# RMS norms of a two-layer diffusion block: sums, roots and reciprocals with tokens on partitions, and two modulation blocks at another place

## Chip, core and metric

The kernel runs on one NeuronCore of one Trainium2 chip. The metric is the device time of one execution in microseconds (us), lower is better. TensorE (PE) multiplies, VectorE (DVE) and ScalarE (ACT) do elementwise work, GpSimd (POOL) and SyncE (SP) issue transfers. In the profile PEld is TensorE's weight load, which overlaps PE.

## Reference

The reference is a two-layer backbone over 512 latent and 256 context tokens of width 1024, all in float32. Cut to what the change touches, it is:

```python
def rms_norm(x, g):
    y = x * rsqrt(mean(x * x, axis=-1) + EPS)
    return y * g

for l in range(2):
    sh1, sc1, g1, sh2, sc2, g2 = split(cond @ w_mod[l] + b_mod[l], 6)   # the modulation; likewise for the context
    u = rms_norm(h, norm1_g[l]) * (1 + sc1) + sh1
    y = token_mixers(u, ...)           # neighbourhood, grouped and differential attention, convolution
    h = h + g1 * (y @ w_out[l])
    u = rms_norm(h, norm2_g[l]) * (1 + sc2) + sh2
    h = h + g2 * expert_choice_ffn(u, ...)   # router, top tokens of each of 16 experts, gated products
return rms_norm(h, final_g)
```

The context tokens take part in layer 0 throughout; in layer 1 they pass only the first norm and the input projection. So the kernel has five norms: the first and second norm of layer 0 and the first of layer 1 over 512 (latent) and 256 (context) tokens where they are needed, the second of layer 1 and the final one over the latent tokens alone.

## The kernel before

**Layout.** The residual stream `h` and the normed `u` keep channels on partitions: 8 slices `k` of 128 channels by 768 tokens (512 latent, then 256 context). The sum over channels of a norm is therefore a sum over partitions. It is made on TensorE: ACT squares a slice into `ex`, and PE multiplies by `ones_d`, a 128x128 matrix of 1/1024, and accumulates the 8 slices in PSUM (`norm_sum`, L543; for the second norm six of the slices are added by DVE first, so that L781 and L784 are two products; `final_sum`, L549). Because every column of `ones_d` is the same, the result has the mean of each token on all 128 partitions. ACT then takes the root of all of it (`norm` of the scalar block, L1051, and L1294 in the final norm), DVE the reciprocal (`invert`, L1356, and L1707), both on 128 partitions by 512 and 256 tokens, and DVE multiplies `h` by the gain and by this array (L1366, L1710: 8 slices of the latent tokens, then 8 of the context). ACT adds the shift (L1063) and PE takes the slices up one after the other: at L599 as the first token tiles of the input projection, at L802 as the router's product.

**Order of work.** Each engine has a program written out by hand. PE's sequence around the second norm of layer 0 is: output projection (L759), the two sum products, the modulation blocks `MOD_N` (numbers 13 and 14), the router (L802, L808), the transposes of `u` for the gather's table in memory (L825), the blocks `MOD_R` (15 to 20), which run beside DVE's search for the top tokens (L1601 to L1605), the transpose of the found rows (L841), the blocks `MOD_G` (21 to 23), and then the first gathered tokens (L863, L866) and the expert products (L886, L892 in layer 0, L880 in layer 1). A modulation block is `mod_products` (L516), a copy on ACT, and `mod_pick` (L527), whose products have a moving operand of 4 columns.

**Weights.** SP loads all weights as blocks of 2 MB in one fixed order (`STREAM`, then the experts' 12 blocks for each pair of experts), each into the next free one of six to nine slots. `fill` (L446) waits until PE has released the slot's last block. So a modulation block that PE takes up later is released later, and so is the slot that the next block in the order needs. For layer 0 the third expert block also waits for the first gather:

```python
if l == 0 and j == 2:
    sp.wait_ge(sig["e_g", 0], 32)
```

The slots of the stretch around the second norm, from the tables of the kernel, are: block 13 in slot 3, 14 in 1, 15 in 4, 16 in 5, 17 in 0, 18 in 2, 19 in 3, 20 in 1, 21 in 4, 22 in 5, 23 in 0, the first two expert blocks in 2 and 3. Slots 4 and 5 lie in attention's buffers and come free when attention is done. Block 18 waits for the last block of the output projection to be released.

**The gather.** GpSimd fetches the tokens of an expert pair with two indirect transfers (`take_rows`, L1757 latent, L1760 context), once DVE has the rows (L1619, L1623). PE transposes what comes (`gather`, L863, L866), ACT copies it out, and the pair's products follow.

## Time and profile before

| | |
|---|---|
| three runs, us | 2116.8, 2120.46, 2122.64 (median 2120.46) |
| the profiled execution, us | 2119.77 |
| its span in the profile, us | 2118.0 |
| mean granted TensorE clock | 0.972 |
| busy in the span: PE, PEld, DVE, ACT, POOL | 91%, 59%, 32%, 24%, 16% |
| HBM read | 506.88 MB |

The span runs from the first to the last profiled instruction; 1.8 us of the execution lie around it. A busy PE is not PE at its peak, since matmuls are pipelined.
### The profile page before, as it was taken

The page shows a single profiled execution, that of the slowest core. Times are in us where ns is not written, and L with a number is a line of the kernel's source. Part 1 is how long each engine was busy: PE and PEld are TensorE (multiplying, and loading weights), DVE is VectorE, ACT ScalarE, POOL GpSimd, SP SyncE. Part 2 cuts the span into 40 slices and gives each one's busy share as a digit, 9 for nine tenths or more (in the row PEclk, how much of TensorE's full clock was granted, in tenths as well). Part 3 has the DMA queues.
Part 4 walks back from the last instruction along what each step waited for, and adds up shares of the span by engine and source line. Part 5 has one row for each costly group of instructions (what it writes and reads, how often), then busy time and mean ns, then how long its engine had stood idle before and what let it go on. Part 6 is the DMA issues. An engine that isn't in the chain of part 4 may idle for free.

```text
span 2118.0 us, 40681 instructions
## 1 busy us (share of the span) xinstructions
PE 1933.4 (91%) x18156; PEld 1247.9 (59%) x18156; DVE 687.1 (32%) x1329; ACT 507.8 (24%) x1118; POOL 344.1 (16%) x200
## 2 busy tenths in 40 slices
PE   6999989989879999999998899979893999988896
PEld 4656656755557666666665546557642666655553
DVE  3085367762520000000002444367635111111113
ACT  4001246640402111211111311246602111110012
POOL 0004037730000111001110004038600000000000
PEclk9999989999989999999999999989996999999999
DMA  9431110062499999999996321110035999999994
GB/s 397 179 137 40 40 40 2 2 266 92 179 378 420 405 401 409 406 411 402 399 387 255 144 75 40 40 41 1 8 153 220 386 426 427 426 428 427 426 428 183
DMA packets 43738, 525.46 MB, mean 248 GB/s; under 512 B 5232, under 2 KB 5232, under 8 KB 13488
## 3 DMA queue, kind: packets, MB, share of 16 engines
q1 hardware_dynamic: 35136, 492.21, 56.2%
q0 software_dynamic: 6992, 25.43, 3.8%
q10 hardware_dynamic: 1440, 5.24, 0.6%
q8 instruction: 144, 2.36, 0.4%
q14 instruction: 26, 0.21, 0.0%
HBM read 506.88 MB, written 15.99 MB: 247 GB/s over the span
## 4 chain that ended last, share of the span: by engine, by line
PE 69%; DMA 11%; DVE 7%; issue 5%; PEld 3%; POOL 2%; ACT 2%; ACTq 0%; SPq 0%; DVEq 0%; PEldq 0%; POOLq 0%
PE ps L886 14%; PE ps L581 12%; PE ps L880 9%; PE ps L892 7%; PE ps L759 6%; PE ps L702 4%; PE ps L599 4%; DMA ring<-in_w_exp 3%; PE ps L1001 2%; PE ps L720 2%; POOL arena L1740 2%; PE ps L736 2%; DMA u<-in_w_exp 2%; DMA arena<-in_w_exp 2%; DVE arena L1515 2%
## 5 line engine op out<-in xcount | busy, mean ns | idle before, releaser
L581 PE MATMUL ps<-u,ring 128*128 128x512 f32 (+1 forms) x800 | 276.9, 507 | 0.0
L1740 POOL TENSOR_SCALAR arena<-arena,rsum 128x768 f32<-128x768 f32 (+3 forms) x120 | 216.5, 1819 | 291.0 <-DVE rsum L1535 241.1
L581 PEld LDWEIGHTS ps<-u,ring 128*128 128x128 f32 x800 | 151.7, 190 | 123.7 <-issue 115.7
L1664 DVE SCALAR_TENSOR_TENSOR arena<-arena,ps 128x512 f32<-128x512 f32 x40 | 27.4, 685 | 538.3 <-ACT arena L1226 538.3
L886 PE MATMUL ps<-ring,arena 128*32 128x256 f32 x3200 | 184.0, 381 | 6.2 <-PE ps L892 3.9
L880 PE MATMUL ps<-ring,arena 128*64 128x256 f32 x1408 | 161.1, 385 | 16.1 <-DMA ring<-in_w_exp 9.4
L880 PE MATMUL ps<-arena 128*64 128x256 f32 x1344 | 151.1, 380 | 13.8 <-DMA arena<-in_w_exp 10.9
L1150 ACT ACTIVATE arena<-arena,negmax 128x768 f32<-128x768 f32 (+3 forms) x160 | 129.8, 812 | 112.2 <-DVE arena L1515 91.4
L886 PEld LDWEIGHTS ps<-ring,arena 128*32 128x32 f32 x3200 | 117.5, 110 | 64.2 <-issue 13.4
L880 PEld LDWEIGHTS ps<-ring,arena 128*64 128x64 f32 x1408 | 105.0, 139 | 70.2 <-DMA ring<-in_w_exp 16.1
L702 PE MATMUL ps<-arena 64*128 64x256 f32 (+4 forms) x576 | 118.2, 518 | 26.9 <-DVE arena L1515 15.5
L759 PE MATMUL ps<-u,ring 128*128 128x512 f32 (+1 forms) x384 | 137.8, 521 | 0.0
L892 PE MATMUL ps<-ring,arena 128*32 128x256 f32 x1600 | 136.9, 382 | 0.0
L880 PEld LDWEIGHTS ps<-arena 128*64 128x64 f32 x1344 | 98.7, 137 | 62.9 <-DMA arena<-in_w_exp 16.9
L886 PE MATMUL ps<-arena 128*32 128x256 f32 x2304 | 132.0, 380 | 0.5 <-PE ps L892 0.5
L892 PE MATMUL ps<-arena 128*32 128x256 f32 x1152 | 129.3, 383 | 0.0
L1226 ACT ACTIVATE arena<-ps 128x512 f32<-128x512 f32 x40 | 24.0, 599 | 438.4 <-PE ps L880 223.4
L599 PE MATMUL ps<-ring,u 128*128 128x256 f32 (+1 forms) x576 | 112.8, 354 | 10.5 <-ACT u L1063 6.1
L1515 DVE TENSOR_SCALAR_CACHE_REDUCE arena<-ps 128x768 f32<-128x768 f32 (+1 forms) x128 | 100.3, 821 | 65.3 <-PE ps L702 64.4
L599 PEld LDWEIGHTS ps<-ring,u 128*128 128x128 f32 x576 | 96.8, 195 | 29.5 <-issue 13.0
L759 PEld LDWEIGHTS ps<-u,ring 128*128 128x128 f32 x384 | 73.0, 190 | 64.5 <-issue 61.2
L886 PEld LDWEIGHTS ps<-arena 128*32 128x32 f32 x2304 | 86.4, 110 | 36.8 <-issue 1.2
(203 smaller groups left out, 2281.5 us busy)
## 6 DMA issues: line engine op xcount, KB each, us to landing
ring<-in_w_exp SPq DMA_DIRECT2D x94, 2048.0 KB
arena<-in_w_exp SPq DMA_DIRECT2D x78, 2048.0 KB, 28.2
ring<-in_w_mod SPq DMA_DIRECT2D x20, 2048.0 KB
u<-in_w_exp SPq DMA_DIRECT2D x20, 2048.0 KB, 28.0
ring<-in_w_in SPq DMA_DIRECT2D x10, 2048.0 KB
ring<-in_w_out SPq DMA_DIRECT2D x4, 2048.0 KB
arena<-in_w_mod SPq DMA_DIRECT2D x4, 2048.0 KB, 11.9
u_rows<-arena ACTq DMA_DIRECT2D x10, 512.0 KB, 2.9
```

What stands on the lines that cost most here:

```text
L581: mm = pe.matmul(ps[:, bb, 0:n], w[:, k, P * ct:P * ct + P], u[:, k, t0:t0 + n], start=k == 0, stop=k == KD - 1)
L599: mm = pe.matmul(ps[:, 4 + nv % 2, 0:cn], u[:, k, P * t:P * t + P], w[:, k, c0:c0 + cn], start=k == 0, stop=k == KD - 1)
L702: mm = pe.matmul(psf[:, c0:c0 + k1 - k0], qk[r0:r0 + rn, qt, q0:q0 + P], qk[r0:r0 + rn, kt, k0:k1], start=True, stop=True, tile_position=( ...
L720: mm = pe.transpose(ps[:, 3 + i % 4, P * x:P * x + P], ex[:, (2 * p + e) % N_EX, P * (y % n):P * (y % n) + P], cst("ident"))
L736: mm = pe.matmul(ps[64 * e:64 * e + 64, 7, 0:P], val[:, kt, v0:v0 + HD], pt[:, i % N_PT, c0:c0 + P], start=x == 0, stop=x == len(ktiles) - ...
L759: mm = pe.matmul(ps[:, 4 + 2 * (i % 2) + c, 0:n], w[:, k, P * (i % 4):P * (i % 4) + P], u[:, k, t0:t0 + n], start=k == 0, stop=k == KD - 1)
L880: mm = pe.matmul(ps[64 * c:64 * c + 64, bank, cols:cols + 256], stationary(k, i), w[i][:, k, 256 * c:256 * c + 256], start=k == 0, stop=k ...
L886: mm = pe.matmul(ps[g:g + 32, bank, cols:cols + 256], stationary(k, i)[:, 32 * r:32 * r + 32], w[i][:, k, 256 * c:256 * c + 256], start=k ...
L892: mm = pe.matmul(ps[g:g + 32, bank, cols:cols + 256], stationary(k, 2 + e), w[e][:, k, 256 * c:256 * c + 256], start=k == 0, stop=k == KD - 1,
L1150: act.activation(ex[:, i % N_EX, 0:kn], ex[:, i % N_EX, 0:kn], ACT.Exp, scale=-1.0, bias=negmax[:, i % 16:i % 16 + 1], accum_out=sums[:, i ...
L1515: dve.tensor_scalar(dst[:, 0:kn], src, -1.0, 3.0e38, ALU.mult, ALU.min, accum_out=low).then_inc(s["s_max"], 1)
L1740: pool.tensor_scalar(e0, e0, rsum[:, c0:c0 + 1], None, ALU.mult).then_inc(s["p_norm"], 1)
```

## The change

It does three things. Each norm's sum is made with the squares as stationary operand, 128 tokens at a time, against 4 columns of `ones_d`, so that the mean of each token lies on its own partition, in one column for every 128 tokens (`token_sums`); ACT's root and DVE's reciprocal then run on 128 partitions by 6 or 4 elements (`inv_t`), and PE spreads each column over all partitions by transposing it, broadcast 128 times (`spread`). DVE's multiplication reads the result from PSUM (`spread_to`). Before the squares of the first norm of each layer and of the final norm ACT takes a root of a constant. And `MOD_N` is gone: blocks 13 to 18 are now `MOD_R`, beside the search for the top tokens, and 19 to 23 are `MOD_G`, after the transpose of the found rows, while the first gather is under way. The order of the loads and their slots is unchanged.

```diff
+        inv_t = mx6
+        def spread_to(c):
+            return ps[:, 0, CTX:CTX + CTX] if c else ps[:, 1, 0:LAT]
...
-        MOD_N, MOD_R, MOD_G = range(13, 15), range(15, 21), range(21, 2 * MOD_BLOCKS)
+        MOD_R, MOD_G = range(13, 19), range(19, 2 * MOD_BLOCKS)
+        MOD_AHEAD = 15
...
-                    if key == ("mod", MOD_R[0]):
+                    if key == ("mod", MOD_AHEAD):
                         sp.wait_ge(sig["dn_sq", 0], 1)
...
+            def token_sums(squares, tiles, start, stop):
+                for t in range(tiles):
+                    mm = pe.matmul(ps[:, 0, 4 * t:4 * t + 4], squares[:, P * t:P * t + P], cst("ones_d")[:, 0:4],
+                                   start=start and t == 0, stop=stop and t == tiles - 1)
+                return mm
-            def norm_sum(which, l, parts, ks=range(KD)):
+            def norm_sum(l, ks=range(KD)):
                 for k in ks:
...
-                    for t0, n, c in parts:
-                        mm = pe.matmul(ps[:, c, 0:n], cst("ones_d"), ex[:, k % 2, t0:t0 + n],
-                                       start=k == 0, stop=k == KD - 1)
-                    mm.then_inc(sig[which + "_mm", l], 1)
+                    token_sums(ex[:, k % 2, :], TL + TC, k == 0, k == KD - 1).then_inc(sig["n1_mm", l], 1)
...
+            def spread(tiles):
+                for t in range(tiles):
+                    mm = pe.transpose(spread_to(t // TL)[:, P * (t % TL):P * (t % TL) + P],
+                                      inv_t[:, t:t + 1].to_broadcast([P, P]), cst("ident"))
+                return mm
...
                 if l == 0:
-                    norm_sum("n1", l, parts_of(l))
+                    norm_sum(l)
+                    pe.wait_ge(sig["n1_inv", l], since("n1_inv", l) + 1)
+                    spread(TL + TC).then_inc(sig["n1_rb", l], 1)
                     pe.wait_ge(sig["cond_done"], 1)
                     modulation(range(4))
...
-                if l == 0:
-                    pe.wait_ge(sig["o_ev", l], KD)
-                    for m in MOD_N:
-                        mod_products(m, 4 + m % 2)
-                    pay()
-                    for m in MOD_N:
-                        mod_pick(m, 4 + m % 2, MOD_TOK["out"][m % 2])
+                pe.wait_ge(sig["n2_inv", l], since("n2_inv", l) + 1)
+                spread(nt).then_inc(sig["n2_rb", l], 1)
...
             def norm(which, l, parts):
...
+                if which == "n1":
+                    act.activation(inv_t[:, 7:8], cst("eps"), ACT.Sqrt)
...
-                act.activation(ex[:, 2, 0:t1], bank2(0, t1), ACT.Sqrt, bias=cst("eps")).then_inc(sig[which + "_root", l], 1)
+                act.activation(inv_t[:, 0:nt], ps[:, 0, 0:4 * nt].rearrange("p (t x) -> p t x", x=4)[:, :, 0], ACT.Sqrt,
+                               bias=cst("eps")).then_inc(sig[which + "_root", l], 1)
...
-                link(dve.reciprocal(ex[:, 2, t0:t0 + n], ex[:, 2, t0:t0 + n]), ("self", l))
+                dve.reciprocal(inv_t[:, 0:nt], inv_t[:, 0:nt]).then_inc(sig[which + "_inv", l], 1)
...
                         dve.scalar_tensor_tensor(u[:, k, t0:t0 + n], h[:, k, t0:t0 + n], gain[:, i, k, c:c + 1],
-                                                 ex[:, 2, t0:t0 + n], ALU.mult, ALU.mult).then_inc(sig[which + "_pre", l], 1)
+                                                 spread_to(c), ALU.mult, ALU.mult).then_inc(sig[which + "_pre", l], 1)
```

The final norm is changed in the same way, with four tiles of tokens.

At the start of the program PE had 16 products of 512 and 256 columns (L543) ahead of the first four modulation blocks (L516, L527); the last two of them head the piece. Before:

```order
L543 MATMUL ps<-arena,const 128x512
L543 MATMUL ps<-arena,const 128x256
L516 MATMUL ps<-ring,cond_w 32x256 x32
L527 MATMUL ps<-const,arena 128x4 x2
L516 MATMUL ps<-ring,cond_w 32x256 x16
```

And now, where L548 is the sum, L564 the spread, L522 and L533 the modulation's products and picks:

```order
L548 MATMUL ps<-const,arena 128x4 x48
L564 MATMUL ps<-const,mx 128x128 x6
L522 MATMUL ps<-ring,cond_w 32x256 x32
L533 MATMUL ps<-const,arena 128x4 x2
L522 MATMUL ps<-ring,cond_w 32x256 x16
```

The spread now stands between the sum and the modulation blocks, and it waits for ACT and DVE.

From the second norm of layer 0 to the first gathered tokens (L863, which is L873 in the change) PE had:

```order
L784 MATMUL ps<-arena,const 128x256
L516 MATMUL ps<-ring,cond_w 32x256 x32
L527 MATMUL ps<-const,arena 128x4 x4
L802 MATMUL ps<-u,small 32x256 x24
L808 MATMUL ps<-const,arena 128x96 x2
...
L841 MATMUL ps<-const,arena 128x48 x4
L516 MATMUL ps<-arena,cond_w 32x256 x32
L527 MATMUL ps<-const,arena 128x4 x2
L516 MATMUL ps<-ring,cond_w 32x256 x16
L527 MATMUL ps<-const,arena 128x4 x4
L863 MATMUL ps<-const,arena 128x128 x4
```

And now (L812 is the router, L851 the transpose of the rows):

```order
L548 MATMUL ps<-const,arena 128x4 x12
L564 MATMUL ps<-const,mx 128x128 x6
L812 MATMUL ps<-u,small 32x256 x24
L818 MATMUL ps<-const,arena 128x96 x2
...
L851 MATMUL ps<-const,arena 128x48 x4
L522 MATMUL ps<-ring,cond_w 32x256 x32
L533 MATMUL ps<-const,arena 128x4 x2
L522 MATMUL ps<-arena,cond_w 32x256 x16
L533 MATMUL ps<-const,arena 128x4 x2
L522 MATMUL ps<-arena,cond_w 32x256 x16
L533 MATMUL ps<-const,arena 128x4 x2
L522 MATMUL ps<-ring,cond_w 32x256 x16
L533 MATMUL ps<-const,arena 128x4 x4
L873 MATMUL ps<-const,arena 128x128 x4
```

Two blocks of 16 products left the place ahead of the router, and five instead of three now stand behind the transpose of the rows.

## Rows read from the trace of the kernel before

**Rows 1.** The page's part 4, the chain that ended last, by engine
```profile
PE 69%; DMA 11%; DVE 7%; issue 5%; PEld 3%; POOL 2%; ACT 2%; ACTq 0%; SPq 0%; DVEq 0%; PEldq 0%; POOLq 0%
```

**Rows 2.** Waits of PE, 612 to 1080 us: engine, waited for, total, times, longest
```profile
PE ps L863 <- issue: 8.4, 1, 8.4
```

**Rows 3.** Chain in order of time, last pairs of layer 1: start us, us, what
```profile
1868.96 36.73 DMA ring<-in_w_exp
...
2087.14 3.70 PE ps L880 x32
```

**Rows 4.** Timeline, short operations: start us, us, engine, line, operation, [idle before]
```profile
569.57 1.04 PE L825 MATMUL ps<-const,u 128*128 128x128 f32 x8
571.30 0.19 DVE L1592 RECIPROCAL mx<-mx 128x6 f32<-128x6 f32 x1
583.05 0.61 PE L527 MATMUL ps<-const,arena 128*128 128x4 f32 x4
```

**Rows 5.** Timeline, start of the program
```profile
14.80 12.90 PE L543 MATMUL ps<-arena,const 128*128 128x512 f32 x32 [14.80 <-ACT arena L1046]
26.03 1.28 ACT L1051 ACT_TABLE_LOAD   x1
27.64 3.66 PE L516 MATMUL ps<-ring,cond_w 128*32 128x256 f32 x64
38.45 8.55 ACT L1063 ACTIVATE u<-u,mod 128x512 f32<-128x512 f32 x16 [1.90 <-DVE u L1366]
39.46 8.86 PE L599 MATMUL ps<-ring,u 128*128 128x256 f32 x32 [2.24 <-DMA ring<-in_w_in]
```

**Rows 6.** One line of the kernel, L543: records, ns min/median/max, first and last start
```profile
L543 PE MATMUL ps<-arena,const x64: 379/592/1193, 14.8 to 1189.7; 128*128 128x512 f32 x32, 128*128 128x256 f32 x32
```

**Rows 7.** Timeline, second norm of layer 0
```profile
551.04 1.56 PE L784 MATMUL ps<-arena,const 128*128 128x512 f32 x4 [0.43 <-ACT arena L1040]
552.64 0.90 ACT L1051 ACTIVATE arena<-ps,const 128x768 f32<-128x768 f32 x1 [1.65 <-PE ps L784]
553.64 3.35 DVE L1356 RECIPROCAL arena<-arena 128x512 f32<-128x512 f32 x1 [3.32 <-ACT arena L1051]
557.03 5.39 DVE L1366 SCALAR_TENSOR_TENSOR u<-h,gain,arena 128x512 f32<-128x512 f32 x8
562.33 1.75 DVE L1356 RECIPROCAL arena<-arena 128x256 f32<-128x256 f32 x1
```

**Rows 8.** Timeline, from the loads of blocks 21 on to the first expert products
```profile
581.75 2.73 SPq L446 DMA_DIRECT2D arena<-in_w_mod  x2
...
600.45 1.93 PE L516 MATMUL ps<-ring,cond_w 128*32 128x256 f32 x32 [2.04 <-DMA ring<-in_w_mod]
...
611.91 1.09 PE L863 MATMUL ps<-const,arena 128*128 128x128 f32 x4 [8.36 <-issue]
...
617.64 8.55 PE L886 MATMUL ps<-ring,arena 128*32 128x256 f32 x128 [1.28 <-issue]
```

**Rows 9.** DMA issues, 595 to 598 us: what, engine, times, us to landing
```profile
arena<-u_rows,rows_c POOLq DMA_INDIRECT x1, 14.6
```

**Rows 10.** Stretches: us, PE, PEld, DVE, ACT, POOL busy, PE clock, DMA share, GB/s
```profile
20.00:25.00 5.00, 5.00 (x17) 2.87 (x16) 0.00 (x0) 3.37 (x4) 0.00 (x0) 1.00 1.00 426
...
606.00:612.00 6.00, 0.09 (x1) 0.12 (x2) 0.00 (x0) 0.00 (x0) 0.00 (x0) 0.55 0.90 273
...
1605.30:1610.20 4.90, 3.72 (x30) 2.86 (x28) 1.58 (x8) 3.15 (x7) 0.00 (x0) 1.00 0.94 399
```

**Rows 11.** Timeline, first norm of layer 1
```profile
1191.13 3.35 DVE L1356 RECIPROCAL arena<-arena 128x512 f32<-128x512 f32 x1 [3.31 <-ACT arena L1051]
...
1205.90 3.29 PE L599 MATMUL ps<-ring,u 128*128 128x256 f32 x14 [0.42 <-ACT arena L1096]
```

**Rows 12.** Timeline, second norm of layer 1 and final norm
```profile
1592.76 0.69 ACT L1051 ACTIVATE arena<-ps,const 128x512 f32<-128x512 f32 x1 [1.22 <-PE ps L784]
...
2109.96 5.39 DVE L1710 SCALAR_TENSOR_TENSOR u<-h,small,arena 128x512 f32<-128x512 f32 x8
```

66 lines of the change are left out of this document (30 added, 36 removed).

## The prediction

> **What bounds the kernel now.** I read the chain of waits first. PE holds 69% of it and transfers 11% [rows 1], so the question of every stage is whether PE or the weight stream ends last. In the experts of layer 0 PE waited for no transfer: its only long idle stretch from 612 us on is the 8.4 us ahead of the first gathered tokens [rows 2]. That stage moves as a whole with its start. In layer 1 the chain of the last pairs hangs on a 36.73 us wait for an expert block, and after the last of these PE has 3.70 us of work [rows 3]: there the stream sets the end, and a gain ahead of it counts only as far as it brings the first release of a slot earlier. The first expert product there releases the first slot, so the second norm of layer 1 still counts. The timeline around each norm then gives the terms. A microsecond there is one at the end unless something covers it.
>
> **The price of the pieces.** A sum of one slice is 12 records now (6 tiles), where it was 4 long ones. Four records with 4 columns take 0.61 us [rows 4], and each further record comes as fast as in a group of transposes, 8 in 1.04 us, so (1.04 - 0.61) / 4 = 0.107 us. Twelve take 0.61 + 8 x 0.107 = 1.47 us, and four of the old records take 1.56 [rows 7]. The sums come out even. The spread is 12 records, 1.04 + 4 x 0.107 = 1.47 us, for six tiles and 1.04 for four. Root and reciprocal of 6 columns: DVE's on 128x6 takes 0.19 [rows 4], and I give ACT the same. From the end of the sum to DVE's first multiplication it was 557.03 - 552.60 = 4.43 us [rows 7]; now it is 0.19 + 0.19 + 1.47 and four hand-overs of 0.1 (553.64 after 552.64 + 0.90), 2.25 in all. **Saved: 2.2 us** for the latent tokens, and 1.75 us more for the context tokens, whose reciprocal [rows 7] stood between the two halves. DVE reads PSUM instead; its operations of this size on PSUM and on SBUF take about the same (5.39 / 8 = 0.67 us for those from SBUF), and I take 0.2 us per norm for it. At the end of a norm with context 3.8 us are saved.
>
> **First norm of layer 0: a loss of 3.3 us.** ACT's table load of 1.28 us stood after the squares, while PE finished its sums (26.03 to 27.31; PE was done at 27.70) [rows 5]. The root of a constant puts it ahead of the first square, with 0.2 us of its own: +1.5. The modulation blocks followed the sums at once, at 27.64 [rows 5]; now the spread stands ahead of them, with root, reciprocal and hand-overs, +2.2. DVE's root and reciprocal were hidden here, so nothing comes back: DVE cannot multiply before the blocks give the gain. The projection's first product waited for its weights until 39.46, some 0.35 us after ACT's first slice (38.45 + 0.67) [rows 5]; that is the only cover. 1.5 + 2.2 - 0.35 = **+3.3**. The weights follow: block 0 is released 3.7 later, and the load behind it starts with an empty queue, but it had been queued behind others before, so it lands before the first slice is ready.
>
> **Second norm of layer 0 and the moved blocks: 0.** All that hangs on the norm comes 3.8 earlier: router, search, the first release of `MOD_R` (581.75 to 577.95 [rows 8]) and the gather. But the stream behind `MOD_R` is longer. Before, SP had loaded blocks 19 and 20 while PE was in the norm; now their slots are freed only in `MOD_R`. A block is 2.10 MB at 426 GB/s [rows 10], 4.93 us. The third block asked for after 581.75 was there at 600.45, when PE went on [rows 8]: 18.7 = 3 x 4.93 + 3.9. The last block of `MOD_G` is now the fifth: 577.95 + 5 x 4.93 + 3.9 = 606.5. The gather's 192 rows of 4 KB (0.79 MB, 1.9 us at that rate) now run beside these loads, which makes it 608.4. Then come the last block's products and picks, 603.56 - 600.45 = 3.1 us, and the gathered tokens' transposes and copies, 617.64 - 611.91 = 5.7 [rows 8]: 617.2 against 617.64. The gather lands earlier: 597.19 - 3.8 + 14.6 = 608.0 [rows 9], and no longer decides. Because the share of the gather could be felt by more than its bytes (its landing took 14.6 us for 1.9 us of bytes), I round the 0.4 of gain away. The two blocks' own 3.66 us on PE cost nothing at either place: ahead of the router PE waited anyway, and now they fall into the 8.4 us of idle.
>
> **First norm of layer 1: -2.8.** DVE starts 2.2 earlier. The third token tile of the projection (1205.90 [rows 11]) waits for ACT, which copies the first tile out only after the last context slice; that is 3.8 earlier, but PE must also do its two first tiles, which start 2.2 earlier and run 0.6 less long once the clock is up. The table load moves to where ACT waits for the experts' last sums.
>
> **Second norm of layer 1: -2.4.** End of sum to multiplication was 1592.73 to 1596.94 (the reciprocal is as long as in [rows 11], the root 0.69 [rows 12]), 4.2; with four tiles it is 0.19 + 0.19 + 1.04 + 0.4 = 1.8.
>
> **Final norm: -2.6.** The same, 4.4 to 1.8; DVE's multiplications started at 2109.96 [rows 12], and all that follows stays.
>
> Sum: +3.3 + 0 - 2.8 - 2.4 - 2.6 = **-4.5 us** on 2119.77, so 2115.3. The profiled execution is 0.7 under the median of the runs; the prediction is **2116.0 us**. About 0.3% (6.4 us) is what a measurement of this kernel can tell from no change, so most of this case lies within it.
>
> **The rivals.**
>
> *A. Slower: the clock stays low through the sums at the start.* The first record of L543 took 1193 ns where the median is 592 [rows 6], so PE begins at its low level (1.2 GHz) and rises to 2.4 while it streams 512 columns without a pause. The new sums stream 4 columns per weight load. If that does not raise the clock, 8 x 12 records take double, 96 x 0.213 = 20.5 us instead of 12.9: +7.6. The spread adds 1.4, and the first two modulation blocks (3.66 us [rows 5]) start low, +2.3. Total 11.3 more: **2127.3**. For it: no row shows a cold PE that rises on such work. Against it: PE would have a record in flight all the time, and in the stretch 1605.30 to 1610.20, which holds only transposes with pauses between, the clock was 1.00 [rows 10]. It decides if the clock does not rise within the first half of the sums. 0.2.
>
> The Trainium skill, page "TensorE: Matmul & The Clock Gate", section "Part 4: PE-mode transpose", says that transposes do not count as busy for the clock. By that rule the four later spreads would run at half the rate, 1.4 + 1.4 + 1.0 + 1.0 = 4.8 us more, and the time would be 2120.8. The stretch just named, with 1.00 over transposes alone, disagrees with it; 0.04.
>
> *B. Faster: the weights are no limit before the first experts.* Then the 3.8 us of the second norm stay. Moreover PE would be at work shortly before the gathered tokens, and not at the 0.55 of the stretch 606 to 612 [rows 10]; the transposes (1.09 us for four records against 1.04 for eight [rows 4, 8]) and the first products would save 1.6. 2116.0 - 5.4 = **2110.6**. It needs the fifth block by 603. Against it is the arithmetic of the queue; for it, that the third block's 3.9 us of delay is one block's reading, and that the gather may share better than I take it. 0.25.
>
> *C. The gather is felt more.* The fifth block lands at 611, not 608.4, because its slowest part waits behind the rows, PE is cold again by then, and the experts start 3 us later: **2119**. 0.15.
>
> *D. The new sums are not even.* If weight loads of squares are not hidden (0.19 us each instead of 0.107), each slice takes 0.8 longer, eight slices at the start and eight before layer 1: 13 more, **2129**. The rows of the four-column picks speak against it. 0.03.
>
> The rest, 0.33, is the forecast itself.
>
> **How the numbers follow.** The forecast's own range is 2112.5 to 2119.5 (the start 1 us either way with the phase of the clock's rise, each norm half a microsecond, the moved blocks two). B reaches below and A above; the range that leaves out no more than 2 in 10 is **2109 to 2127.5**. Faster by over 0.3% is below 2114.1: nearly all of B and a quarter of the forecast, 0.32. Slower is over 2126.8: 0.6 of A, D, and a little of C, 0.17. The rest is 0.51.
>
> **What would show it.** In the profile after: DVE's first multiplication 2.2 us after the last sum of a norm with six tiles and 1.8 with four; a table load before the first square and the projection's first product at 42.8; the last block's products ahead of the first gathered tokens at about 608, ended by a transfer; layer 1's projection 2.8 nearer to its last sum; in the last layer the first release of a slot 2.4 nearer to the norm. A span of PE records of 20 us at the start shows A. A first expert product before 616 (617.64 with the 3.3 of the start is 620.9) shows B. The prediction is wrong if the start loses nothing, or if the expert stage of layer 0 begins to wait for transfers.

## The result, and the profile after

The changed kernel takes **2135.14 us** (median of 5 runs, 2131.4 to 2138.47), the kernel before beside it 2120.46: ratio 1.0070, 95% interval 1.0055 to 1.0084. It is slower by 0.7%, outside the forecast range (2109 to 2127.5). On two other chips (runs e12 and e16 below) it came out at 1.0062 both times (2135.83 and 2134.40 us).

| | before | after |
|---|---|---|
| profiled execution, us | 2119.77 | 2135.14 |
| its span, us | 2118.0 | 2133.3 |
| mean granted clock | 0.972 | 0.968 |
| PE busy in the span | 91% | 92% |

The chain by engine has lost DVE time, 5% for 7% [rows 1], as the change meant, but PE and transfers have more.

```profile
PE 71%; DMA 12%; DVE 5%; issue 5%; PEld 3%; POOL 2%; ACT 2%; ACTq 0%; SPq 0%; DVEq 0%; PEldq 0%; POOLq 0%
```

**The start.** The timeline of the changed kernel, which answers to [rows 5]. L548 is the sum, L1066 the root, L564 the spread, L522 the modulation products, L617 the projection:

```profile
13.53 1.28 ACT L1048 ACT_TABLE_LOAD   x1
...
15.90 20.61 PE L548 MATMUL ps<-const,arena 128*128 128x4 f32 x96 [15.90 <-ACT arena L1061]
...
36.55 0.27 ACT L1066 ACTIVATE mx<-ps,const 128x6 f32<-128x6 f32 x1 [4.28 <-PE ps L548]
36.91 0.19 DVE L1373 RECIPROCAL mx<-mx 128x6 f32<-128x6 f32 x1 [22.64 <-ACT mx L1066]
...
37.16 1.54 PE L564 MATMUL ps<-const,mx 128*128 128x128 f32 x6 [0.65 <-DVE mx L1373]
38.63 5.77 PE L522 MATMUL ps<-ring,cond_w 128*32 128x256 f32 x64
...
52.41 1.20 PE L617 MATMUL ps<-ring,u 128*128 128x256 f32 x3 [2.10 <-ACT u L1076]
```

The 96 records of the sums take 20.61 us, 0.213 each, where 0.107 was worked out, and the modulation products behind them 5.77 instead of 3.66. The projection's first product comes at 52.41 instead of 39.46: 12.95 us of the 15.3 by which the spans differ are lost before anything else has begun. The durations of the records show that the engine was at its low level, 1.2 GHz, until about 43 us; the column PEclk, the granted clock, does not:

```profile
core 0: us, PE busy (x) PEld busy (x) DVE busy (x) ACT busy (x) POOL busy (x), PEclk, DMA share, GB/s
...
20.00:24.00 4.00, 4.00 (x21) 4.00 (x20) 0.00 (x0) 1.09 (x2) 0.00 (x0) 1.00 0.98 418
```

Twenty-one records in 4 us, all of it busy, are the low rate, and beside it stands 1.00; e5 below has 1.00 beside 21 records in 4 us and then beside 38. So at the start of an execution a reader goes by the duration of the records and not by this column.

**The second norm of layer 0.** This answers to [rows 7]; DVE's multiplication is L1381.

```profile
566.13 1.47 PE L548 MATMUL ps<-const,arena 128*128 128x4 f32 x12
568.09 2.29 PE L548 MATMUL ps<-const,arena 128*128 128x4 f32 x12 [0.49 <-ACT arena L1055]
570.42 0.27 ACT L1066 ACTIVATE mx<-ps,const 128x6 f32<-128x6 f32 x1 [2.38 <-PE ps L548]
570.79 0.19 DVE L1373 RECIPROCAL mx<-mx 128x6 f32<-128x6 f32 x1 [3.41 <-ACT mx L1066]
...
571.03 1.54 PE L564 MATMUL ps<-const,mx 128*128 128x128 f32 x6 [0.65 <-DVE mx L1373]
572.62 2.72 DVE L1381 SCALAR_TENSOR_TENSOR u<-h,gain,ps 128x512 f32<-128x512 f32 x4 [1.64 <-PE ps L564]
```

The first twelve records take the 1.47 us of the forecast. In the second twelve the clock falls, and they take 2.29. From their end (570.38) to the multiplication it is 2.24 us, and the forecast was 2.25. The spread in it is six records, one for each tile, not the twelve of the forecast, and they run at the low level: 1.54 us, where six take 0.87 at the full clock (e5 and e15 below).

**From there to the experts.** The chain, and PE's timeline, which answer to [rows 8]:

```profile
605.34 21.72 DMA ring<-in_w_mod
```
```profile
627.11 3.36 PE L522 MATMUL ps<-ring,cond_w 128*32 128x256 f32 x32 [2.90 <-DMA ring<-in_w_mod]
...
636.40 1.08 PE L896 MATMUL ps<-ring,arena 128*32 128x256 f32 x8 [1.12 <-issue]
```

The last modulation block lands 21.7 us after it was asked for (13.9 before), and the experts start at 636.40, 18.8 us behind before's 617.64.

**Layer 1 and the end.** The first norm of layer 1 (the first two rows), its second norm and the final norm answer to [rows 11, 12]:

```profile
1213.94 0.19 DVE L1373 RECIPROCAL mx<-mx 128x6 f32<-128x6 f32 x1 [2.72 <-ACT mx L1066]
...
1215.83 3.38 DVE L1381 SCALAR_TENSOR_TENSOR u<-h,gain,ps 128x512 f32<-128x512 f32 x5 [1.70 <-PE ps L564]
```
```profile
1612.62 0.26 ACT L1066 ACTIVATE mx<-ps,const 128x4 f32<-128x4 f32 x1 [1.15 <-PE ps L548]
...
1614.37 5.36 DVE L1381 SCALAR_TENSOR_TENSOR u<-h,gain,ps 128x512 f32<-128x512 f32 x8 [1.21 <-PE ps L564]
```
```profile
2125.30 5.36 DVE L1722 SCALAR_TENSOR_TENSOR u<-h,small,ps 128x512 f32<-128x512 f32 x8 [1.21 <-PE ps L564]
```

The delay against the kernel before, read from both timelines at the same instructions: first product of the projection +12.95 us, first attention product +15.39, output projection +17.0, first expert product +18.76, first wide scatter product +23.15, layer 1's first transposed projection tile +19.98, expert stage of layer 1 +17.04, final multiplication +15.34. So the stretches that hold the two norms of layer 1 and the final one gain (3.2, 2.9 and 1.7 us), and all others lose. Between the first expert product and the first wide scatter product of layer 0, where the change has edited nothing on PE, the delay grows by 4.4 us.

### The profile page after: what moved, and what is told of

It reads as the page before. It is cut to its first block, busy times and chain, and to the rows that moved or that the text cites. A ratio compares the mean times of both kernels' runs of the same rounds, so it can differ in the third digit from the quotient of the medians.

```text
span 2133.3 us, 41142 instructions
## 1 busy us (share of the span) xinstructions
PE 1957.4 (92%) x18386; PEld 1277.7 (60%) x18386; DVE 665.6 (31%) x1326; ACT 505.7 (24%) x1121; POOL 342.3 (16%) x200
## 4 chain that ended last, share of the span: by engine, by line
PE 71%; DMA 12%; DVE 5%; issue 5%; PEld 3%; POOL 2%; ACT 2%; ACTq 0%; SPq 0%; DVEq 0%; PEldq 0%; POOLq 0%
PE ps L896 14%; PE ps L599 12%; PE ps L890 9%; PE ps L902 7%; PE ps L777 6%; PE ps L617 4%; PE ps L720 4%; DMA ring<-in_w_exp 3%; PE ps L1011 2%; PE ps L738 2%; PE ps L548 2%; POOL arena L1752 2%; PE ps L754 2%; DMA u<-in_w_exp 2%; DMA arena<-in_w_exp 2%
## 5 line engine op out<-in xcount | busy, mean ns | idle before, releaser
L896 PEld LDWEIGHTS ps<-ring,arena 128*32 128x32 f32 x3200 | 116.8, 111 | 65.4 <-issue 13.7
L617 PE MATMUL ps<-ring,u 128*128 128x256 f32 (+1 forms) x576 | 112.0, 352 | 5.5 <-ACT u L1076 3.8
L617 PEld LDWEIGHTS ps<-ring,u 128*128 128x128 f32 x576 | 96.3, 194 | 24.3 <-issue 8.6
```

Of the source, the lines that this page charges most:

```text
L617: mm = pe.matmul(ps[:, 4 + nv % 2, 0:cn], u[:, k, P * t:P * t + P], w[:, k, c0:c0 + cn], start=k == 0, stop=k == KD - 1)
L896: mm = pe.matmul(ps[g:g + 32, bank, cols:cols + 256], stationary(k, i)[:, 32 * r:32 * r + 32], w[i][:, k, 256 * c:256 * c + 256], start=k ...
```

## The experiments

Two theories stood at the beginning. **Theory 1:** the loss is the start; the sums of 4 columns do not raise the clock, and root, reciprocal, spread and table load stand in series. **Theory 2:** the loss lies in the moved blocks and the transfers behind them. Ratios are against the kernel before on the same chip. "Scatter to tile" is the time from the first 512-column scatter product to layer 1's first transposed projection tile, in which the first norm of layer 1 lies; it and the two starts are from the one profiled execution. Each group of runs was made on one chip: e1 to e4, e5 to e8, e9 to e12, and e13 to e16; the kernel before has one median for the first result and one for each of these groups.

| run | median us | ratio (interval) | projection starts | L0 experts start | scatter to tile |
|---|---|---|---|---|---|
| before | 2120.5; 2121.7, 2122.3, 2122.4, 2121.4 | 1 | 39.5 | 617.6 | 50.7 |
| changed (first / e12 / e16) | 2135.1 / 2135.8 / 2134.4 | 1.0070 / 1.0062 / 1.0062 | 52.4 / 52.6 / 51.9 | 636.4 / 635.7 / 634.9 | 47.5 / 53.9 / 47.5 |
| e1 old first norm | 2125.17 | 1.0011 (0.9999, 1.0023) | 39.5 | 620.3 | 58.9 |
| e2 PE warmed ahead | 2136.88 | 1.0079 (1.0063, 1.0095) | 50.2 | 630.9 | 47.6 |
| e3 blocks back | 2137.38 | 1.0073 (1.0057, 1.0089) | 52.5 | 633.0 | 47.5 |
| e4 = e1 and e3 | 2120.87 | 0.9997 (0.9984, 1.0009) | 39.7 | 621.2 | 55.6 |
| e5 128 columns | 2118.04 | 0.9985 (0.9973, 0.9997) | 41.7 | 621.4 | 46.9 |
| e6 e5, start reordered | 2117.31 | 0.9981 (0.9972, 0.9991) | 39.9 | 619.7 | 46.9 |
| e7 e6, blocks back | 2111.53 | 0.9952 (0.9938, 0.9965) | 40.2 | 621.1 | 47.0 |
| e8 e4, 128 columns | 2109.07 | 0.9940 (0.9927, 0.9953) | 39.7 | 623.4 | 46.9 |
| e9 before, blocks moved | 2130.13 | 1.0031 (1.0019, 1.0044) | 39.3 | 623.4 | 50.7 |
| e10 128 columns at the start only | 2131.26 | 1.0044 (1.0030, 1.0058) | 42.0 | 627.0 | 53.9 |
| e11 start reordered, 4 columns | 2133.81 | 1.0059 (1.0045, 1.0072) | 48.5 | 631.4 | 47.6 |
| e13 128 columns but at the start | 2127.12 | 1.0033 (1.0021, 1.0045) | 52.5 | 631.6 | 46.9 |
| e14 blocks back, once more | 2133.84 | 1.0058 (1.0038, 1.0078) | 51.9 | 635.0 | 53.9 |
| e15 e5, blocks back | 2114.79 | 0.9964 (0.9951, 0.9977) | 42.6 | 622.9 | 46.9 |

### e1: the first norm of layer 0 as before

```
+                    if l == 0:
+                        for t0, n, c in parts_of(l):
+                            mm = pe.matmul(ps[:, c, 0:n], cst("ones_d"), ex[:, k % 2, t0:t0 + n],
+                                           start=k == 0, stop=k == KD - 1)
...
-                    spread(TL + TC).then_inc(sig["n1_rb", l], 1)
```

> The changed kernel, with the first norm of layer 0 put back as it was before the change (ones times 512 columns, root and reciprocal of 768 columns, no spread); the other four norms and the moved modulation blocks stay changed. Theory 1 (the start is the loss: the four-column sums run at 1.2 GHz and the spread and table load stand in series): the projection's first product is back at about 39.5 us instead of 52.41, everything behind it is at least 12.9 us earlier, 2135.1 - 12.9 = 2122, and nearer 2118 if the 2.4 us more at 97 to 131 us and the 1.7 us more in the attention only come from the shifted phase of the clock. Theory 2 (the loss lies in the stretch of the moved blocks and behind it, where the transfers set the time, and the start's delay would be absorbed there): the experts of layer 0 start hardly earlier than 636.4, and the time stays above 2130.

Measured: 2125.17 us, ratio 1.0011, and the projection starts at 39.55. About ten of the fifteen us come back, so theory 1 has the main part, but not the 13 to 17 that it forecast, and theory 2 falls as the main cause. The new thing is in the last column: 58.9 us from scatter to tile, 8 more than before the change, in a stretch that theory 1 held for won.

### e2: a warm PE ahead of the sums

```
+                    for i in range(12):
+                        pe.matmul(ps[:, 7, :], cst("ones_d"), const[:, 0:512], start=True, stop=True)
                     norm_sum(l)
```

> The changed kernel with 12 matmuls of ones times 512 columns of the constants into an unused bank of PSUM, on PE ahead of its first sum, in the 9.9 us in which it waited for the input. Nothing else differs, so this changes the clock alone. Theory 1a (the clock is the larger part of the start's loss, and four-column sums hold a clock that is up): the 96 records of the sums take about 10.5 us instead of 20.61, the products of the first modulation blocks 3.66 instead of 5.77, the projection's first product comes at about 40.5 instead of 52.41, and the time is about 2123. Theory 1b (four-column sums let even a raised clock fall): the sums start at 0.107 us a record and turn to 0.213 on the way, and the gain is 2 to 6 us, 2129 to 2133. Theory 2 (the start's delay is absorbed later): same as the changed kernel, 2135.

The stretches of this kernel around its sums, which run from 18.47 to 34.12:

```profile
14.00:18.00 4.00, 4.00 (x10) 1.71 (x9) 0.29 (x2) 2.54 (x4) 0.00 (x0) 1.00 1.02 438
...
20.00:22.00 2.00, 2.00 (x20) 2.00 (x20) 0.00 (x0) 1.50 (x2) 0.00 (x0) 1.00 1.03 442
22.00:24.00 2.00, 2.00 (x19) 2.00 (x19) 0.00 (x0) 1.01 (x3) 0.00 (x0) 0.94 1.00 426
24.00:26.00 2.00, 2.00 (x11) 2.00 (x10) 0.00 (x0) 0.77 (x1) 0.00 (x0) 0.50 0.99 426
...
30.00:32.00 2.00, 2.00 (x11) 2.00 (x11) 0.00 (x0) 0.00 (x0) 0.00 (x0) 0.50 0.88 377
```

The wide products raise the clock; the sums begin at it, twenty records in 2 us, and at 23.8 us (the 0.94 of its stretch), with PE busy in 2.00 of 2.00 us and a record always in flight, it falls to the low level and stays there to the end of the sums. That is the mechanism of theory 1b: these records, though the profile counts them as busy, do not hold the clock. Its time did not come: the projection starts 2.2 us earlier (50.16), but the median, 2136.88, is not below the changed kernel's, where 2129 to 2133 was forecast. The profiled execution (2129.75) is the fastest of the six, and it would be wrong to read a gain from it. Because the fall came here from a clock that was up, it may come in other long rows of such records too.

### e3 and e4: the blocks back, alone and with the old first norm

```
-        MOD_R, MOD_G = range(13, 19), range(19, 2 * MOD_BLOCKS)
+        MOD_N, MOD_R, MOD_G = range(13, 15), range(15, 21), range(21, 2 * MOD_BLOCKS)
...
+                    for m in MOD_N:
+                        mod_products(m, 4 + m % 2)
```

> The changed kernel with the two modulation blocks (13 and 14) put back into the second norm of layer 0, behind its spread; all five norms stay changed. Theory 1 (the start is the loss, and the blocks' move costs what the ledger of the traces shows, the 3.1 us that the norm had gained and 1.7 more): the experts of layer 0 start 3 to 5 us earlier than 636.40, and the time is 2130 to 2132. Theory 2 (the moved blocks are the main loss): more than 8 us faster, under 2127. Theory 3 (the stream of weights sets the experts' start whichever stage the two blocks are in): within 1 us of 2135.1.

> Both edits at once: the first norm of layer 0 and the two modulation blocks as before the change, the other four norms changed. Theory 1: the loss of the start goes (13 to 17 us) and that of the blocks too (3 to 5), which leaves the gains of the later norms, 2135.1 - 15 - 4 = 2116, and 2112 to 2119 in all; this would be faster than the kernel before (2120.5) by the norms' 2.9 + 2.9 + 1.7 us and what the second norm of layer 0 keeps. Theory 2 (the later norms gain nothing net): equal to the kernel before, 2120.5.

e3 gained nothing (1.0073), as only the third theory had it; but that theory's reason, that the weights set the experts' start at either place, does not fit, since the experts start 3.4 us earlier in its profile (633.04), itself the fastest of its six executions. e4 only equals the kernel before (0.9997), the time of its theory 2, although four of its norms are shorter. Its scatter-to-tile stretch took 55.6 us. In e12, a further execution of the changed kernel, the same stretch can be seen in rows. PE's timeline there, L1023 being the wide scatter product:

```profile
1199.04 1.02 PE L1023 MATMUL ps<-arena 128*128 128x512 f32 x2
1199.90 2.74 PE L548 MATMUL ps<-const,arena 128*128 128x4 f32 x24
...
1203.98 2.56 PE L548 MATMUL ps<-const,arena 128*128 128x4 f32 x12
...
1209.10 7.68 PE L548 MATMUL ps<-const,arena 128*128 128x4 f32 x36
```
```profile
1200.00:1204.00 4.00, 4.00 (x30) 3.36 (x29) 1.14 (x2) 1.68 (x2) 0.00 (x0) 0.97 1.02 438
1204.00:1208.00 4.00, 4.00 (x16) 3.56 (x15) 1.14 (x2) 0.84 (x1) 0.00 (x0) 0.50 0.13 53
```

Twenty-four records take 2.74 us, then the clock falls within the sums and 36 take 7.68, which are 4.08 where it does not fall. Of ten profiles with four-column sums in layer 1, five show this (e1, e4, e10, e12, e14), and scatter to tile takes 53.9 to 58.9 us in them, 47.5 to 47.6 in the other five. In those five the clock was lost too, only later: the spread right behind the sums ran at the low level in all ten, 1.51 to 1.52 us for its six records. The first changed profile:

```profile
1214.27 1.51 PE L564 MATMUL ps<-const,mx 128*128 128x128 f32 x6 [0.74 <-DVE mx L1373]
```

### e5: 128 columns instead of 4

```
-                    mm = pe.matmul(ps[:, 0, 4 * t:4 * t + 4], squares[:, P * t:P * t + P], cst("ones_d")[:, 0:4],
-                                   start=start and t == 0, stop=stop and t == tiles - 1)
+                    mm = pe.matmul(psf[:, P * t:P * t + 128], squares[:, P * t:P * t + P], cst("ones_d")[:, 0:128],
+                                   start=start and t % TL == 0, stop=stop and t in (TL - 1, tiles - 1))
```

> The changed kernel with 128 columns of ones instead of 4 as the moving operand of every sum (each tile's sum stands 128 times in PSUM; the root reads one column of each). Nothing else differs. The transposes of the spread, 128 columns each, take 0.107 us a record at 2.4 GHz as the four-column sums do, so the sums should cost the same at that level. Theory 1 (four columns leave the clock low at the start, and let it fall in the sums of layer 1; 128 columns raise and hold it): the sums at the start take about 13 us instead of 20.61, the projection's first product comes at about 43 instead of 52.41, the 24 records of the sums of layer 1 take 2.7 us in whatever execution is profiled, and the time is 2115 to 2120, some 17 us under the changed kernel. Theory 2 (any group of short records with a weight load each leaves the clock low, however wide): start as in the changed kernel, 20.6 us, and the time stays at 2135. Theory 3 (128 columns cost twice as much as 4): the sums take over 20 us at either level, and the time is 2135 or more.

The start of this kernel:

```profile
15.98 12.60 PE L548 MATMUL ps<-const,arena 128*128 128x128 f32 x96 [15.98 <-ACT arena L1061]
29.23 0.87 PE L564 MATMUL ps<-const,mx 128*128 128x128 f32 x6 [0.65 <-DVE mx L1373]
30.03 3.66 PE L522 MATMUL ps<-ring,cond_w 128*32 128x256 f32 x64
...
41.71 9.30 PE L617 MATMUL ps<-ring,u 128*128 128x256 f32 x32 [2.10 <-ACT u L1076]
```

and its stretches there:

```profile
16.00:20.00 4.00, 4.00 (x21) 4.00 (x22) 0.00 (x0) 1.42 (x2) 0.00 (x0) 1.00 0.98 418
20.00:24.00 4.00, 4.00 (x38) 4.00 (x38) 0.00 (x0) 2.43 (x3) 0.00 (x0) 1.00 1.02 438
```

The same 96 records with the same weight loads. The first four microseconds hold 21 of them, as in the changed kernel; the next four hold 38 where that one holds 21. Thirty-two times the columns cost nothing (12.60 us, against 20.61) and the clock rises. The median is 2118.04 us, as theory 1 had it (2115 to 2120), 17 under the changed kernel and faster than the kernel before by 0.15% (0.03 to 0.27). Theories 2 and 3 fall. The last 36 records of layer 1's sums, and the spread behind them:

```profile
1193.46 4.18 PE L548 MATMUL ps<-const,arena 128*128 128x128 f32 x36
...
1198.38 0.84 PE L564 MATMUL ps<-const,mx 128*128 128x128 f32 x6 [0.74 <-DVE mx L1373]
```

That is 4.18 us in each of the six profiles with 128 columns there (e5 to e8, e13, e15), and scatter to tile takes 46.9 to 47.0: no fall in the sums in six of six, where four columns had it in five of ten, and the spread at the full clock (0.84 us) in six of six, where it was at the low one in ten of ten.

### e6 and e7: the serial rest of the start, and the blocks

```
-                if which == "n1":
+                if which == "n1" and l:
                     act.activation(inv_t[:, 7:8], cst("eps"), ACT.Sqrt)
...
                     norm_sum(l)
-                    pe.wait_ge(sig["n1_inv", l], since("n1_inv", l) + 1)
-                    spread(TL + TC).then_inc(sig["n1_rb", l], 1)
                     pe.wait_ge(sig["cond_done"], 1)
                     modulation(range(4))
+                    pe.wait_ge(sig["n1_inv", l], since("n1_inv", l) + 1)
+                    spread(TL + TC).then_inc(sig["n1_rb", l], 1)
```

> The kernel with sums of 128 columns, and two more edits at the start: the root of a constant ahead of the first square only in layer 1, and the spread behind the first four modulation blocks instead of ahead of them. Theory 1 (the remaining loss of the start is serial: 1.5 us for the table load, 2.2 for the spread): the projection's first product comes at 39.5 to 40.5, 3 us ahead of the kernel with 128 columns alone, and the time is 2 to 3 us under it. Theory 2 (this loss is absorbed by the waits for weights behind it): the same time as with 128 columns alone.

> As the kernel before this one, and the two modulation blocks back in the second norm of layer 0. Theory 1 (moving the blocks gave back the 3 us that the second norm had gained, since the queue of weights ends later): 1 to 4 us faster than with the blocks moved, the experts of layer 0 starting 2 us or more ahead of 617.64. Theory 3 (the blocks' place makes no difference): the same within 1 us.

The order brings the projection's start from 41.71 to 39.87, but only 0.7 us of time with overlapping intervals: between its two theories e6 decides nothing. The blocks' return is worth 5.8 us, and the intervals (0.9972 to 0.9991, 0.9938 to 0.9965) do not touch; that is more than the 1 to 4 that e7 forecast. Its profile shows it elsewhere than expected: the experts start at 621.1 where e7 forecast less than 615.6. From the start of the output projection to the first expert product it is 1.6 us shorter than in e6, and from there to layer 0's scatter 2.8 us.

### e8: e4 with 128 columns

> The kernel with the first norm of layer 0 and the two blocks as before the change, now with sums of 128 columns in the other four norms. With four columns it came out equal to the kernel before (2120.87 us against 2121.7), though its later norms are shorter; in its profiled execution the clock fell in the sums of layer 1, and the stretch from the scatter to the projection lost 5 us. Theory 1 (this fall is what ate the norms' gain): with 128 columns the sums of layer 1 run at 2.4 GHz throughout, and the time is 4 to 7 us under the four-column version, 2114 to 2117. Theory 2 (the fall there comes by chance with any kind of sum): equal to it, 2121.

2109.07 us, ratio 0.9940: the same kernel with 128 for 4 columns in four norms is 11.8 us faster than e4, more than the 4 to 7 of theory 1 (they ran on different chips; by the ratios it is 12.1). It is the fastest of the study, **0.6% under the kernel before** (0.47 to 0.73). Its profiled execution (2116.48) is the slowest of its six, so nothing is read here from its stages alone. Against e7 (2111.53) the intervals overlap: with 128 columns the old and the new first norm of layer 0 can't be told apart.

### e9 to e12: each part by itself

> The changed kernel itself, as the measure for the three runs beside it: 2134 to 2137 us, ratio 1.007 as before. If the loss at the start is fixed and only the falls of the clock in the sums of layer 1 come by chance, its runs should lie in two heaps some 8 us apart.

> The changed kernel with sums of 128 columns in the first norm of layer 0 alone; the other four norms keep 4 columns. Theory 1: the start gives back 10.7 us (the projection's first product at 41.7), the falls of the clock in the sums of layer 1 stay possible, so the time is 10 to 12 us under the changed kernel, 2124 to 2126, and some 6 us above the 2118 of the kernel with 128 columns in all norms. Theory 2 (the start is the whole of the clock's cost): 2118, as with 128 columns in all norms.

> The changed kernel, sums of 4 columns, with the root of a constant ahead of the first square only in layer 1 and the spread behind the first four modulation blocks. This takes away the serial part of the start's loss alone. Theory 1 (serial 3.3 us, the clock the other 9 to 10): the projection's first product at 49 to 50 instead of 52.41, and 2 to 4 us faster than the changed kernel. Theory 2 (the start's loss is serial in the main): more than 8 us faster.

> The kernel before with only the two modulation blocks moved; all five norms as before. Theory 1 (the last block of the gather's wait lands some 22 us after it is asked for instead of 14, because two more blocks are queued, and the norm gives nothing to pay for it): the experts of layer 0 start at 620 to 623 instead of 617.64, and the time is 2 to 5 us over the kernel before, 2124 to 2126. Theory 3 (the blocks' place makes no difference): within 1 us of the kernel before. Theory 4 (in the old place their products and copies lay on the path to the router): 1 to 3 us faster than before.

e12's six runs (2129.0, and 2134.1 to 2138.5) are no two heaps, and its profile with the fall is as long as the first one without: the fall in layer 1 is one of several that move between executions.

e10 takes 128 columns at the start alone. The projection starts at 42.0, yet only 4.6 us come back, and its interval still overlaps that of e12. In its profile the clock fell again behind the start, in the second norm of layer 0, ahead of the experts and in the sums of layer 1:

```profile
556.00:566.00 10.00, 7.75 (x36) 5.23 (x38) 5.29 (x9) 4.59 (x8) 0.00 (x0) 0.51 0.45 185
611.00:631.00 20.00, 15.75 (x120) 9.33 (x116) 0.46 (x5) 2.51 (x6) 1.86 (x2) 0.50 1.00 416
```

The second of these stretches begins in the gather's wait, where the kernel before has a low stretch too (0.55 [rows 10]), and whether the narrow sums have a part in it no run shows. e11, the serial part alone, gives some 4 us at the projection's start and 2.0 in the median, where 2 to 4 were expected; the intervals of e11 and e12 overlap almost wholly, so that the 2.0 are not shown.

e9 was made from the kernel before: its old norms, and the two blocks in the gather's wait. Forecast 2 to 5 us over the kernel before, measured 7.7 by the medians and 6.6 by the ratio (1.0031, interval 1.0019 to 1.0044): four of its eleven executions lie at 2123.1 to 2126.5 and seven at 2129.4 to 2133.0, and the profiled one is of the seven. PE's timeline, L517 being the modulation product, L880 the expert product:

```profile
607.66 3.64 PE L517 MATMUL ps<-arena,cond_w 128*32 128x256 f32 x32 [3.93 <-DMA arena<-in_w_mod]
...
614.05 3.40 PE L517 MATMUL ps<-ring,cond_w 128*32 128x256 f32 x32 [1.80 <-DMA ring<-in_w_mod]
...
623.40 8.81 PE L880 MATMUL ps<-ring,arena 128*32 128x256 f32 x124 [1.12 <-issue]
```

against e7, where the blocks are back (its modulation product is L522, its first transpose of gathered tokens L880):

```profile
603.36 3.62 PE L522 MATMUL ps<-ring,cond_w 128*32 128x256 f32 x32 [1.91 <-DMA ring<-in_w_mod]
...
615.48 1.08 PE L880 MATMUL ps<-const,arena 128*128 128x128 f32 x4 [7.33 <-issue]
```

With the blocks moved the gathered tokens follow the last block's products at once, and PE waits for that block; with the blocks back PE has idled for 7.33 us when the tokens come. The last block lands 22.4 us after it is asked for in e9, 13.7 in e7 and 13.9 in the kernel before. The queue has become the limit of this stage.

### e13 to e16: width by place on one chip

> The changed kernel with sums of 128 columns in every norm but the first of layer 0, which keeps 4. Theory 1a (the clock in the later sums costs as much as at the start, by falls in the two long rows of short records, layer 1's first norm above all, and in the second norm of layer 0 ahead of the router): with 128 columns at the start alone 4.6 us came back of 17.7, so here 10 to 13 us come back, 2123 to 2126. Theory 1b (what the start lost is lost however the rest runs, and the 4.6 us were small by the chance of the clock's falls behind it): 5 us or less come back, 2130 to 2133.

> The changed kernel with the two blocks back in the second norm of layer 0, sums of 4 columns, once more beside the changed kernel itself. Theory 1 (the blocks' place costs 6 us at any width, hidden in the first run by few runs and another chip): 4 to 7 us faster than the changed kernel beside it. Theory 2 (with four columns the sums of the second norm let the clock fall ahead of the router, and the blocks' products behind the spread then run at the low level and hold the router up, which eats the gain): the same as the changed kernel within 2 us.

> Sums of 128 columns in all norms, the two blocks back in the second norm of layer 0, the order at the start as in the changed kernel. With the other order at the start the blocks' return gave 5.8 us (2117.31 to 2111.53). Theory 1: the same here, 2118.0 - 5.8 = 2112, ratio to the kernel before 0.9955. Theory 2 (it hung on the order at the start): 2116 or more.

> The changed kernel itself on the chip of the three runs beside it: 2135 to 2137 us, ratio 1.006 to 1.007.

128 columns everywhere but at the start (e13) give 7.3 us of the changed kernel's 2134.4, at the start alone (e10) 4.6, everywhere (e5) about 17. Neither of e13's theories is met. By these medians the parts do not add, but each has an interval of two to three us to either side and they come from three chips, so that this is not shown; it may be that what one place gains another loses while four-column sums are left somewhere. Blocks back with four columns (e14) again give nothing, 0.6 us; with 128 columns (e15 against e5) 0.9985 becomes 0.9964, some 4.5 us, though these intervals just overlap; with e6 and e7 it is 5.8. e15's median, 2114.79, lies between its two theories (2112, and 2116 or more). Theory 2 of e14 fits, and the second norm of layer 0 shows its mechanism. With four columns (e14):

```profile
567.13 2.64 PE L548 MATMUL ps<-const,arena 128*128 128x4 f32 x12 [0.49 <-ACT arena L1062]
570.43 1.54 PE L564 MATMUL ps<-const,mx 128*128 128x128 f32 x6 [0.65 <-DVE mx L1383]
571.90 4.71 PE L522 MATMUL ps<-ring,cond_w 128*32 128x256 f32 x64
```

and with 128 (e15):

```profile
557.36 1.60 PE L548 MATMUL ps<-const,arena 128*128 128x128 f32 x12 [0.39 <-ACT arena L1062]
559.61 0.87 PE L564 MATMUL ps<-const,mx 128*128 128x128 f32 x6 [0.65 <-DVE mx L1383]
560.41 3.66 PE L522 MATMUL ps<-ring,cond_w 128*32 128x256 f32 x64
```

The clock falls in the second group of narrow sums, and the spread and the blocks' products ahead of the router run at the low level: 2.64 + 1.54 + 4.71 = 8.89 us against 6.13. What the blocks' return saves behind the router is lost ahead of it. From the output projection's start to the router it is 95.5 us in e14 against 89.5 in e16, where the blocks are moved, and from the router to the experts 57.3 against 63.0: 6.0 lost, 5.8 gained. With 128 columns it is 92.7 (e15) against 89.6 (e5) and 57.7 against 62.0: 3.1 lost, 4.4 gained. That this is the whole reason for e14's equal median is not shown: its profile also has the fall in layer 1's sums, 6.4 us in scatter to tile, which that of e16 does not have.

## Why the prediction was wrong

**"First norm of layer 0: +3.3".** This step failed, and rival A describes what came instead: the clock stays low through the sums. Its 96 x 0.213 = 20.5 us were measured as 20.61, its products of the first blocks (+2.3) as +2.1, and the start as a whole lost 12.95 where A gives 14.6. The serial terms themselves were near: with 128 columns, when the clock rises, the start loses 2.25 to 3.09 (e5, e10, e15), not 3.3.

A had a chance of 0.2, and the argument against it was the error. I took the 1.00 over a stretch of transposes [rows 10] for a sign that short records hold the clock. Those moved 128 columns each and the sums moved 4, and e5 shows what that difference does: its sums are the same records with 128. And "PE would have a record in flight all the time" is no argument: in e2 PE was 100% busy while its clock fell. The row that should have decided is [rows 6]: in the kernel before only records of 512 and 256 columns had been seen to raise it.

**The sums are even.** At the full clock that holds: 1.47 us a slice as worked out (566.13). D is refuted.

**The price of the pieces.** 2.25 us from sum to multiplication with six tiles and 1.8 with four; 2.24 and 2.30, and 1.79 twice, were measured in the first profile. That is luck: two errors cancel. The spread was priced as twelve records at the full clock (1.47 us); it is six, and they ran at the low level (1.54). The note under the profile before, that x8 at a transpose means four of them, is wrong: a transpose has one record (L825 runs 80 of them in the kernel before, and 80 records stand there), and only the other products have two. At the full clock six take 0.87 us, and the whole distance is 1.56 in the second norm of layer 0 of e5, and 1.32 with four tiles. Its final norm, whose sums end at 2106.36:

```profile
2107.69 5.36 DVE L1722 SCALAR_TENSOR_TENSOR u<-h,small,ps 128x512 f32<-128x512 f32 x8 [0.74 <-PE ps L564]
```

So the later norms were worth 0.5 to 0.7 us more each than forecast, and the narrow sums took it away.

**"Second norm of layer 0 and the moved blocks: 0".** This step failed too. The stage from output projection to experts lost 1.7 us in the first profile, 4.0 and 1.0 in the two others (e12, e16). With 128 columns it lost 0.2 and 0.3 (e5, e6). The queue's arithmetic stands: first request 595.73 + 30.45 (577.95 to 608.4) gives 626.2, and the last block's products began at 627.11. Its judgement did not: I set the loss of the longer queue off against the norm's gain and called it zero, though the two blocks cost 6.6 to 7.7 us alone (e9) and 4.5 to 5.8 with all norms shortened at 128 columns. Moving them was a loss, not a zero, and the sum should have held both terms. A part of the cost comes after the experts have started: from the first expert product to the first wide scatter product of layer 0 it is 550.5 to 552.8 us in the seven profiles with the blocks at the old place, and 552.9 to 555.9 in the eleven with them moved. The two stretches together give 5.5 + 1.7 us in e9 against the kernel before, 1.6 + 2.8 in e6 against e7 and 1.2 + 3.4 in e5 against e15, which is near the medians. What in the expert stage takes the longer is open, and the forecast, by which that stage moves as a whole with its start, had no term for it.

**Rival A's total.** A gave 2127.3, and 2135.1 came. It priced the clock only at the start. e13 shows what it left out: with the start as slow as ever, 128 columns in the other norms give 7.3 us, and 2127.12 is nearly A's own number. That is in part luck, since A too put the moved blocks at nothing.

**Layer 1 and the end, -2.8, -2.4, -2.6.** In the first profile -3.2, -2.9 and -1.7. The first holds only when the clock does not fall in the sums: e12 has +3.2 in its place. For the last, the clock fell in the sums ahead of it (their last 24 records took 3.60 us, 2.99 in e5) and the spread ran at the low level (1.21 us of wait for it, 0.74 in e5); with 128 columns it is -2.5.

**The Trainium skill's rule on transposes** (page "TensorE: Matmul & The Clock Gate", section "Part 4: PE-mode transpose") was given 2120.8. In the changed kernel's profile the four later spreads did run at the low level, as that rival had it (1.54, 1.51, 1.11 and 1.12 us), but in e5 the same transposes took 0.87, 0.84, 0.65 and 0.65, the full rate. So the sums ahead of them made the difference, not the transposes. Whether transposes count for the clock no run here tells.

**B and C.** B's 2110.6 is not reached with the blocks moved in any execution; with the blocks back and 128 columns it nearly is (2111.5, 2109.1). C needed the fifth block 2.6 us late; it was 0.9 late.

**What is left open.** From the start of the projection to that of the output projection the changed kernel lost another 4.1 us, and e12 0.9 with the same code. Besides that of the kernel before there are seventeen profiles. Nine of them, the first changed one among them, have a low stretch of the clock that begins 3 to 5 us ahead of the output projection. These nine lose 2.4 to 6.7 us on the way there against the kernel before and the other eight 0.4 to 1.4, with narrow sums and with wide, so it is no matter of the sums' width. Which of the two brings the other is open. The read-back of the rows ahead of the scatter took 29.90 us in the first profile and 26.92 in e12 (26.40 before); PE waited 8.0 us for it in the first, 4.5 before. It took 29.3 to 31.3 us in six of the eleven profiles with the blocks moved, and at most 27.5 in all seven without; no run was made for it.

## What to carry to other kernels

Replacing few wide matmuls by many narrow ones at equal PE time is not neutral where they run in a long row: price them at both levels of the clock, and try wider moving operands before giving them up: 128 columns cost here what 4 did at the same clock (36 records 4.18 us against 4.08), and 96 records that began at the low level took 12.60 us instead of 20.61. A wait that seems free to fill has a queue behind it; list how many blocks must land before its end, and keep their cost and the gain that is meant to pay for it as two terms. Where executions of one kernel differ by up to 12.6 us (e1), decide by the medians of many, and take from one profile only durations and order. A measured stage that equals its forecast is not yet a step that held: look at the count and the rate of the records in it.

## What the runs showed of the hardware

- PE at 2.00 us busy of 2.00, with four columns a record and a weight load for each, falls from 2.4 to 1.2 GHz (e2, at 23.8 us) and does not rise in 20.6 us from the low level. The same records with 128 columns rise (e5, 21 records in 4 us, then 38) and hold (36 in 4.18 us in six of six).
- A record of 128 columns and one of 4 take nearly the same time at the full clock, each with a weight load of 128 columns: 36 in 4.18 and 4.08 us.
- A float32 transpose stands in the trace as one record (L825: 80 for 80, L564: 6 for 6), another float32 product as two (96 for the 48 of the sums). Six transposes take 0.87 us at the full clock and 1.54 at the low one.
- Ahead of the first change of the clock in an execution, the profile's clock column shows 1.00 while the records run at half the rate (the changed kernel and e5, 21 in 4 us).
